# Turning the feed-forward's h with 16 block transposes on the vector engine in place of four turns on TensorE

## What is computed

```
x = x + 1/2 * SwiGLU_1(RMSNorm(x))
h = RMSNorm(x); mixers A, B, C and three gates from h @ w_in; merged; x = x + merged @ w_out
x = x + 1/2 * SwiGLU_2(RMSNorm(x))
SwiGLU(x) = (silu(x @ w_gate) * (x @ w_up)) @ w_down      # D_MODEL 1024, D_FF 2816
```

## Time and profile before

| | before |
|---|---|
| median of 3 runs | 1245.17 us (1244.53 to 1245.95) |
| the profiled execution's own time | 1245.35 us |
| its span in the trace | 1243.5 us |
| busy over the span: PE, its weight loads, DVE, ACT, POOL | 98%, 80%, 62%, 51%, 6% |
| granted TensorE clock, mean over the span | 0.995 |
| DMA | 220.83 MB, 178 GB/s |

### The profile page before, as it was taken

How to read it: one execution, slowest core, us unless ns; L and a number is a source line. 1 busy time by engine, 2 the same in 40 slices (tenths; PEclk the granted TensorE clock), 3 DMA queues, 4 the chain that set the end, 5 groups by cost and what they waited for, 6 DMA issues and landing times.

```text
span 1243.5 us, 17453 instructions
## 1 busy us (share of the span) xinstructions
PE 1224.3 (98%) x6016; PEld 993.7 (80%) x6016; DVE 768.5 (62%) x1456; ACT 637.9 (51%) x1079; POOL 72.1 (6%) x151
## 2 busy tenths in 40 slices
PE   7999999999999999999999999999999999999996
PEld 6888888887777888888888888888877778888885
DVE  5555556657767775555575555575677686655555
ACT  5444445656665464444454444455676735444442
POOL 4300000420000000000000000024000000000000
PEclk8999999999999999999999999999999999999999
DMA  8645553543344554554565554544433354555553
GB/s 319 231 174 194 202 192 146 183 164 134 104 136 147 192 177 176 202 202 175 196 221 185 202 200 173 201 151 164 149 122 128 111 202 138 215 202 186 185 187 134
DMA packets 31586, 220.83 MB, mean 178 GB/s; under 512 B 3504, under 2 KB 4144, under 8 KB 5552
## 3 DMA queue, kind: packets, MB, share of 16 engines
q1 hardware_dynamic: 30384, 214.60, 48.2%
q10 hardware_dynamic: 1120, 5.57, 1.3%
q0 software_dynamic: 32, 0.00, 0.0%
HBM read 218.58 MB, written 1.05 MB: 177 GB/s over the span
## 4 chain that ended last, share of the span: by engine, by line
PE 97%; DVE 1%; DMA 1%; ACT 0%; issue 0%; ACTq 0%; SPq 0%; DVEq 0%
PE G L1242 23%; PE G L1244 23%; PE G L1243 23%; PE O L1244 3%; PE O L1242 3%; PE O L1243 3%; PE SC L1243 3%; PE SC L1244 3%; PE SC L1242 3%; PE T L1416 3%; PE SC L1426 2%; PE T L1319 2%; PE O L1477 2%; PE T L1258 1%; DVE wlo L853 1%; DMA raw<-stream 1%
## 5 line engine op out<-in xcount | busy, mean ns | idle before, releaser
L853 DVE TENSOR_TENSOR wlo<-raw,whi 128x1024 fp32r<-128x1024 f32 x398 | 471.5, 1227 | 291.4 <-ACT whi L512 291.1
L512 ACT ACTIVATE whi<-raw 128x1024 fp32r<-128x1024 f32 x398 | 399.1, 1053 | 250.0 <-PE G L1244 125.1
L1242 PE MATMUL G<-whi,xhi 128*128 128x512 f32 x1184 | 468.5, 396 | 4.4 <-DVE xlo L877 4.4
L1244 PE MATMUL G<-whi,xlo 128*128 128x512 f32 x1184 | 459.1, 388 | 0.0
L1243 PE MATMUL G<-wlo,xhi 128*128 128x512 f32 x1184 | 458.4, 387 | 0.0
L1242 PEld LDWEIGHTS G<-whi,xhi 128*128 128x128 f32 x1184 | 223.0, 188 | 52.2 <-DVE wlo L853 4.6
L1244 PEld LDWEIGHTS G<-whi,xlo 128*128 128x128 f32 x1184 | 222.9, 188 | 46.5
L1243 PEld LDWEIGHTS G<-wlo,xhi 128*128 128x128 f32 x1184 | 223.3, 189 | 42.4
L570 ACT ACTIVATE shared_q<-G,stat 128x256 f32<-128x256 f32 x88 | 41.8, 475 | 170.2 <-PE G L1244 166.6
L922 DVE SCALAR_TENSOR_TENSOR shared_q<-shared_q,G 128x256 f32<-128x256 f32 x88 | 36.8, 418 | 100.4 <-ACT shared_q L570 100.4
L665 ACT ACTIVATE probs<-sm,stat 128x256 f32<-128x256 f32 (+2 forms) x128 | 51.9, 407 | 53.5 <-DVE stat L1048 53.5
(11 more groups left out here) (170 smaller groups left out, 989.3 us busy)
## 6 DMA issues: line engine op xcount, KB each, us to landing
raw<-stream SPq DMA_DIRECT2D x201, 1024.0 KB, 4.8
gates<-w_in ACTq DMA_DIRECT2D x2, 2048.0 KB, 8.7
x<-x_in SPq DMA_DIRECT2D x2, 512.0 KB, 7.5
out<-x SPq DMA_DIRECT2D x4, 256.0 KB, 2.0
small<-small_in ACTq DMA_DIRECT2D x2, 414.5 KB, 3.4
const<-const_in SPq DMA_DIRECT2D x1, 689.0 KB, 13.8
z<-final_in SPq DMA_DIRECT2D x1, 512.0 KB, 3.5
kvcT<-kvcT ACTq DMA_DIRECT2D x2, 255.0 KB, 3.2
```

The lines of the kernel that those rows point to most:

```text
L512: act.activation(whi[s][:, c : c + PART], raw[s][:, c : c + PART], ACT.Copy).then_inc(hi_done, 1)
L853: dve.tensor_tensor(wlo[s][:, c], raw[s][:, c], whi[s][:, c].bitcast(F32), ALU.subtract).then_inc(lo_done, 1)
L1242: pe.matmul(o, ahi, bhi, start=first, stop=False)
L1244: return pe.matmul(o, alo, bhi, start=False, stop=last)
```

## The change

On PE the calls of `turn_h` for chunks 0 to 9 of each stage go; that of the last chunk stays. DVE gets a new `turn_h(g)` in their place: 16 transposes, each over 32 partitions and 128 elements of each (four blocks of 32 x 32, for two halves of the tokens and two halves of the channels), from `h` into `hT`, another part of the tile `shared_q`. ACT rounds `hT` (`round_h`), and DVE subtracts from `hT` (`rest_of_h`), both later in the round than before: DVE's round becomes swiglu(g, 0), split 3i+2, swiglu(g, 1), split 3i+3, turn_h(g), split 3i+4, rest_of_h. The diff, cut:

```diff
+        hT = shared_q[:, 1024:1536].rearrange("p (k t) -> p k t", k=2)
...
-                def turn_h(n, j=0):
+                def round_h(n, j, turned):
                     act.wait_ge(ht_filled, n)
-                    act.activation(hThi[j].rearrange("p k t -> p (k t)"), T[0][:, :], ACT.Copy).then_inc(ht_hi_done, 1)
+                    act.activation(hThi[j].rearrange("p k t -> p (k t)"), turned, ACT.Copy).then_inc(ht_hi_done, 1)
...
                 with act.Fori(1, FI - 1) as i:
                     g = o * FI + i
                     swish(g, 0, None)
-                    turn_h(g)
                     split_in_loop(l, i, at, 2)
                     swish(g, 1, l * LAYER_UNITS + i * RING + at)
                     split_in_loop(l, i, at, 3)
                     split_in_loop(l, i, at, 4)
+                    round_h(g + 1, 0, by_dve)
...
+                def turn_h(g):
+
+                    dve.wait_ge(h_done, g * 2 + 2)
+                    blocks = h.rearrange("p t (k c j) -> p t k c j", k=2, c=4)
+                    turned = hT.rearrange("p k (t r i) -> p t k r i", t=TOKS, r=4)
+                    for r in range(4):
+                        for c in range(4):
+                            ins = dve.transpose(
+                                turned[32 * c : 32 * c + 32, :, :, r, :], blocks[32 * r : 32 * r + 32, :, :, c, :])
+                    ins.then_inc(ht_filled, 1)
+
+                def rest_of_h(n, j, turned):
                     dve.wait_ge(ht_hi_done, n)
                     dve.tensor_tensor(
-                        hTlo[j].rearrange("p k t -> p (k t)"), T[0][:, :],
+                        hTlo[j].rearrange("p k t -> p (k t)"), turned,
                         hThi[j].rearrange("p k t -> p (k t)").bitcast(F32), ALU.subtract,
                     ).then_inc(ht_lo_done, 1)
...
                 swiglu(o * FI, 1, steps.then)
+                turn_h(o * FI)
                 split(l, at, 4)
+                rest_of_h(o * FI + 1, 0, by_dve)
                 with dve.Fori(1, FI - 1) as i:
...
                     swiglu(g, 0, steps.then)
-                    turn_h(g)
                     split_in_loop(l, i, at, 2)
                     swiglu(g, 1, steps.then)
                     split_in_loop(l, i, at, 3)
+                    turn_h(g)
                     split_in_loop(l, i, at, 4)
+                    rest_of_h(g + 1, 0, by_dve)
...
                 gate_up(1, 0)
-                turn_h(o * FI + 1)
                 gate_up(1, 1)
                 down(o * FI + 1, l * LAYER_UNITS, at + 4, first=True)
                 with pe.Fori(2, FI - 1) as i:
                     gate_up(i, 0)
-                    turn_h(o * FI + i)
                     gate_up(i, 1)
                     down(o * FI + i, l * LAYER_UNITS + i * RING, at + 1)
                 last = FI - 1
                 gate_up(last, 0)
-                turn_h(o * FI + last)
                 gate_up(last, 1)
```

More of the change, by code:

```diff
@@ L572, in swish @@
                     )
-                def turn_h(n, j=0):
+                def round_h(n, j, turned):
                     act.wait_ge(ht_filled, n)
-                    act.activation(hThi[j].rearrange("p k t -> p (k t)"), T[0][:, :], ACT.Copy).then_inc(ht_hi_done, 1)
+                    act.activation(hThi[j].rearrange("p k t -> p (k t)"), turned, ACT.Copy).then_inc(ht_hi_done, 1)
+                by_dve = hT.rearrange("p k t -> p (k t)")
                 act.wait_ge(rstd_done, lift_of(l, 2 * occ) + 1)
@@ L595, in ffn @@
                 split(l, at, 4)
+                round_h(o * FI + 1, 0, by_dve)
                 with act.Fori(1, FI - 1) as i:
@@ L609, in ffn @@
                 split(l, at, 3 * last + 3)
-                turn_h(o * FI + FI, 1)
+                round_h(o * FI + FI, 1, T[0][:, :])
                 if (l, occ) != (L - 1, 1):
@@ L968, in ffn @@
                 split(l, at, 3 * last + 3)
-                turn_h(o * FI + FI, 1)
+                rest_of_h(o * FI + FI, 1, T[0][:, :])
                 if (l, occ) != (L - 1, 1):
```

## The result

The changed kernel takes 1225.75 us, median of four runs (1225.23 to 1226.32), against 1244.85 for the kernel before in the same set of runs: a ratio of 0.9847 (95% interval 0.9835 to 0.9858), 19.1 us less. Forecast were 1225.9 us and 19.4 us less. The profiled execution took 1226.32 us, its span is 1224.5.

What follows compares the result with a forecast made beforehand. The prediction took PE's stream as the bound: 40 turns at 0.485 us take 19.4 us off the profiled 1245.35 us, with DVE's added transposes hidden, giving 1225.9 us; range 1223.5 to 1231.5 us.

Steps and rivals of the forecast that it cites:

- The bound: Whole kernel: PE's stream sets the time, busy throughout a 16.82 us round, while DVE idles 7.5 us of it.
- The removed term: On PE, 40 turns of four transposes leave the stream at 0.485 us each, 19.4 us in all.
- the slower dozen: The dozen matmuls behind each turn on PE, over which the last 0.05 us of its 0.49 us cost is spread.
- rival (c): On PE, only the 0.36 us up to the next matmul goes per turn: 14.4 us saved, 1230.8 us; chance 0.04.
- (d): On PE, the transposes' durations are the saving: 43 us, giving 1202 us; chance 0.01.
- The added term: On DVE, 16 transposes a chunk at 0.30 us, 4.8 us, making 14.1 us of a 16.32 us round, hidden.
- X: Step from start to start of one DVE transpose, taken as 0.30 us.
- The block's fill: On DVE, a 32 x 32 block must be filled before being read; if that doubles the passes, 418 ns a transpose.
- The margins: Time to spare before PE's `down`: 1.0 us at the fourth stage's first chunk, 5.0 us in later rounds.
- (a): First chunk of each stage stalls, DVE transpose step between 0.364 and 0.438 us: 3.1 us in all, 1229.0 us; chance 0.09.
- (b): DVE becomes the bound from a transpose step of 0.47 us; at 0.54, rounds of 18.0 us, 1293 us; chance 0.08.
- The queues: ACT's rounding waits for DVE's turn, moving nothing in its queue, some 600 ns from SBUF; late DVE fetch about 1 us.

Runs made afterwards that it cites:

- run 13: Not a label: "that run" is the changed kernel with the whole DVE turn done twice (32 transposes), 1354.91 us; 13 counts its gaps followed by the lower clock.

## Why the prediction was right

**The bound.** PE's stream alone set the end, and still does: without any turn the kernel takes the same 1225.6 us.

**The removed term.** Forecast were 40 x 0.485 = 19.4 us; 19.1 were measured, 0.477 a turn. The stage shows the same: from its first swiglu to its last subtraction the fourth took 168.53 us before and takes 163.75, 4.78 less for ten turns. The choice was between 0.36 up to the next matmul, 0.44 with the one behind, and the 0.49 of whole rounds; the starts in the changed kernel are regular at 0.2267 us, so the slower dozen belonged to the turn, and rival (c) falls. So does (d): four transposes of 271 ns took 0.48 us from PE's stream and not 1.08. The duration that the Trainium skill gives ("TensorE: Matmul & The Clock Gate", Part 4: PE-mode transpose), about 275 ns in a kernel, agrees with the 271 ns of the row, and neither is a price.

**The added term.** X was taken as 0.30, between 0.22 and 0.42; it is 0.316, of which 303 ns are the duration. The block's fill doubles nothing. That the 0.30 came so near is partly luck: it was taken from the duration of another operation, while the step turned out to be 0.198 us where no group changes, below the forecast's lower end of 0.22, and 0.12 more where one does. The round on DVE is 9.16 + 16 x 0.316 = 14.2 us against the 14.1 forecast. Since it is hidden, both turns together gave 1244.6 against 1244.5.

**The margins.** Forecast were 1.0 us at the first chunk of the fourth stage for X = 0.30; 0.7 were there, which is the 0.26 that 16 steps of 0.316 add. In the later rounds the forecast had 5.0 us and 4.3 are there (67.57 to 71.89): it took the 0.49 of the turn ahead off DVE's times and not off the 56.30 that it counted PE's next `down` from, and the turn is the same 0.26 longer. 20 transposes broke the first chunk's margin. The limits in X of rivals (a) and (b), 0.364, 0.438 and 0.47, are in transposes of 0.316 us 18.4, 22.2 and 23.8. With 20 came the stall at the first chunk (2.6 us, 3.1 forecast for X = 0.42, 1.7 for this run), with 24 a time above the kernel before (by 0.6%), with 32, whose 10.1 us are more than the 8.7 of (b), 129 us more. So (a) and (b) were real mechanisms, and the chip's step lay below both. But the forecast's sum for (b) was too low. At its limit of 0.47 the kernel should have been as fast as before, and with 24 transposes, which lie there, it took 8 us more: the sum counted the rounds alone and left out the stall at the first chunk and the wait for the last chunk's h.

**The queues.** ACT's rounding waits 74 us in all for the turn and holds nothing up. The waits for loads are the same few before and after; ACT's for a weight unit is a single one of 7.7 us in both. DVE's longer loop body showed no late fetch: with 24 transposes, where DVE is the bound, its round of 16.71 us is filled from start to start. ACT's rounding from SBUF took 633 ns, not 600, in covered time.

## What to carry to other kernels

Price work that leaves a saturated PE by the distance between starts in a stretch with and without it, not by its duration. Give it to another engine where that engine's round, summed by steps, stays below PE's, and look for the tightest due time at a stage's first and last rounds, not in the middle. Keep on PE whatever would come late there: a gap of 3 us at a stage's end cost the gap and the lower clock behind it.

## What the runs showed of the hardware that was not expected

A short DVE instruction on 32 partitions steps by 0.20 us where both groups of partitions stay and by 0.316 where one of them changes from one instruction to the next, over 128 elements of float32. With gaps counted from start to start less one step, those of up to 1.9 us (24 transposes, at the first `down` of a stage) left the granted clock at 1.0, with a mean of 0.996. Behind the four of 2.9 us and the four of 4.5 us (the last chunk on DVE) it went to the 1.2 GHz level each time, for 3.2 to 4.4 us, beginning at the restart or up to 1.3 us after it. With 32 transposes the mean is 0.971, and gaps of nearly one size did not all do the same:

```profile
78.54 0.39 PE L1267 MATMUL G<-whi,xlo 128*128 128x512 f32 x1
81.58 0.49 PE L1265 MATMUL SC<-whi,ybhi 128*128 128x512 f32 x1 [2.66 <-DVE yblo L948]
81.91 0.40 PE L1266 MATMUL SC<-wlo,ybhi 128*128 128x512 f32 x1
...
97.80 0.39 PE L1267 MATMUL G<-whi,xlo 128*128 128x512 f32 x1
100.83 0.79 PE L1265 MATMUL SC<-whi,ybhi 128*128 128x512 f32 x1 [2.64 <-DVE yblo L948]
101.42 0.63 PE L1266 MATMUL SC<-wlo,ybhi 128*128 128x512 f32 x1
101.84 0.63 PE L1267 MATMUL SC<-whi,yblo 128*128 128x512 f32 x1
```

Both gaps are 2.8 us; behind the first the matmuls keep the fast step, behind the second they start every 0.43 us. Of the 21 gaps of 2.7 to 2.8 us in that run 13 were followed by the lower clock and 8 were not; the four of 4.2 to 4.4 us all were, and the 13 of 1.1 to 1.4 us never. So the size of a gap doesn't decide by itself, and what does was not tried. I had expected that a moderate gap costs only itself.
